# Order of root, reciprocal, table load and weight rounding around the norms of a two-block network

## Chip, core and metric

The kernel runs on one core of a Trainium2 chip. The metric is the device time of one execution in microseconds (us). The engines are called PE (TensorE; PEld is its weight load), DVE (VectorE), ACT (ScalarE), POOL (GpSimd) and SP (SyncE, which here issues most DMAs). Each engine runs its own list of instructions in order, and semaphores tie the lists together.

## What is computed

Two transformer-like blocks on a sequence of 512 tokens of width 1024, all in float32. The first block (differential attention, Fourier mixing and a routed mixture of experts) isn't touched. The second one has two layers; each is a mixer (layer 0: an S5 state-space mixer, layer 1: Mamba-2) and a squared-ReLU MLP, with a modulated RMS norm ahead of each and one at the end:

```python
def _rmsnorm(x, g):
    return x * lax.rsqrt(jnp.mean(x * x, axis=-1, keepdims=True) + NORM_EPS) * g
def _sq_relu_mlp(h, w1, w2):
    a = jax.nn.relu(h @ w1)
    return (a * a) @ w2

for i in range(2):
    sh1, sc1, g1, sh2, sc2, g2 = split(silu(c) @ ada_w[i] + ada_b[i])
    h = _rmsnorm(x, norm_mix_g[i]) * (1 + sc1) + sh1
    y = s5_mixer(h) if i == 0 else ssd_mixer(h)      # Mamba-2; its end: y = groupwise rmsnorm(y * silu(z)) @ w_out
    x = x + g1 * y
    h = _rmsnorm(x, norm_mlp_g[i]) * (1 + sc2) + sh2
    x = x + g2 * _sq_relu_mlp(h, mlp_w1[i], mlp_w2[i])
return _rmsnorm(x, final_norm_g)
```

## The kernel before

Activations lie with features on the 128 partitions: `x`, `h` and the like are eight chunks (KC = 8) of 128 features by T = 512 tokens. Large products of the second block are made of three matmuls for each pair of chunks: weights and activations are each split into a rounded high part and a low rest, and high*high, low*high and high*low are added in PSUM (L739, L742 and L743; L759, L762 and L763 for the first half tile of a pass, which goes chunk by chunk). The high part of a weight tile is made by ACT (`round_half`, one instruction for half a tile, 128x2048, recorded at L1497), the low one by DVE (`split_weight_half`, L2076), which waits for ACT's. A tile has two halves, and there are two tiles in the ring (s = 0, 1); SP loads them as PE frees them.

Norms are numbered k. Norms 5 to 8 belong to the second half: 5 stands ahead of the MLP of layer 0, 6 ahead of the Mamba-2 input projection ("xbc"), 7 ahead of the MLP of layer 1, 8 is the last one. They run so:

- ACT squares the chunks of `x` as DVE finishes them (`norm_squares`, L1503; for norm 5 inside the S5 output loop, L1845, and the last two in `mlp`, L1852). DVE adds the squares of chunks up (`add_square`, L2040).
- PE sums over features in `joined_sum` (L784), then drains and signals `ms_done`.
- ACT takes the root (`norm_root`, L1509) straight from PSUM, 128x128 in size. Ahead of it stands a root of a single column (L1506), the first instruction that needs the table of the root; where another table is in place, a table load is recorded in front of it, at its line.
- DVE takes the reciprocal (`norm_inverse`, L2029), and PE spreads it over the partitions with eight small matmuls (L790).
- DVE scales a chunk (`scaled` in `split_normed`, L2086), ACT adds the shift and rounds it (`norm_shift_rounded`, L1524), DVE makes the low rest (L2097), and PE starts on that chunk. Chunk after chunk follows while PE works.

The weights of the first tile are rounded and split in the same place. ACT's order is: squares, both halves of the tile (`round_weights`), table and root, shifts. DVE's order in `split_normed` is: split of the first half, reciprocal, wait for the spread, scalings; the second half is split behind chunk 4.

In the Mamba-2 output (`m2_out`) the normed values come in four groups of four chunks. DVE scales a group (L2804), ACT copies it rounded (the four copies recorded at L1497), DVE subtracts (L2807, `lo_ready`), and PE uses four chunks of rows for each half tile. ACT rounds the second tile, both halves, ahead of group 1's copies. The order on every engine is written out by hand.

## Time and profile before

| | us |
|---|---|
| median of 3 runs | 2343.35 |
| the runs | 2343.03, 2343.35, 2350.75 |
| the profiled execution | 2343.23 |
| its span | 2341.50 |

The profile is of one execution. The span goes from its first instruction to its last; 1.73 us lie around it. A matmul's duration overlaps the next one's, and ACT and DVE instructions overlap their successors by about 0.1 us, so a start time tells more than an end. In a timeline, what stands in brackets is the engine's idle time ahead of the instruction and the work that ended it. PEclk is the clock granted to PE, 1.00 being full speed (2.4 GHz) and 0.50 half (1.2 GHz).

### The profile page before, as it was taken

What the parts mean: (1) busy time and instruction counts of PE and PEld (TensorE: products, weight loads), DVE (VectorE), ACT (ScalarE), POOL (GpSimd) and SP (SyncE); (2) the same over time, 40 slices, a digit from 0 to 9 for tenths busy, and PEclk for the clock granted to TensorE, in tenths of its full rate; (3) what the DMA queues carried; (4) which work ended last, traced back from release to release, by engine and by line L of the source; (5) the groups of instructions that cost most, each with busy time, mean ns of one, the idle gap of its engine ahead of it and who ended that gap; (6) DMA issues with size and microseconds to landing.
All of it is one profiled execution on the core that took longest, in us unless ns stands there. A gap on an engine that the chain in (4) does not pass through costs nothing.

```text
span 2341.5 us, 23672 instructions
## 1 busy us (share of the span) xinstructions
PE 2092.8 (89%) x9320; PEld 1387.1 (59%) x9320; DVE 1123.0 (48%) x1607; ACT 674.2 (29%) x1029; POOL 162.8 (7%) x172
## 2 busy tenths in 40 slices
PE   6999997987777877979899999899779898999998
PEld 2544443322222226657688888787557686888886
DVE  1866853120111107884465565577684464433434
ACT  3123422110100106213232232243663423322321
POOL 0011101023000023000000000000120000000000
PEclk9999998999999999989899999999889998999999
DMA  9746565999999994212344455223433122322321
GB/s 389 281 145 220 200 256 173 401 429 426 427 428 427 427 390 153 82 63 72 126 171 162 170 172 166 95 90 126 149 105 108 55 90 72 105 93 90 107 90 54
DMA packets 119377, 455.81 MB, mean 195 GB/s; under 512 B 8844, under 2 KB 18096, under 8 KB 104056
## 3 DMA queue, kind: packets, MB, share of 16 engines
q1 hardware_dynamic: 92856, 369.85, 41.6%
q0 software_dynamic: 21312, 76.36, 9.3%
q10 hardware_dynamic: 5120, 8.39, 1.0%
q8 instruction: 60, 0.98, 0.2%
q14 instruction: 29, 0.24, 0.0%
HBM read 436.88 MB, written 21.06 MB: 196 GB/s over the span
## 4 chain that ended last, share of the span: by engine, by line
PE 69%; DMA 18%; DVE 7%; ACT 3%; DVEq 2%; issue 1%; SPq 0%; POOL 0%; ACTq 0%; PEldq 0%; PEld 0%; POOLq 0%
PE PS L739 14%; PE PS L743 14%; PE PS L742 14%; DMA work<-in_w_gu 10%; PE PS L825 4%; PE PS L1111 4%; DMA ring<-in_w_gu 3%; PE PS L1130 3%; DMA work<-in_ada_w_2T 3%; PE PS L954 2%; PE PS L1239 2%; PE PS L759 2%; PE PS L762 2%; PE PS L763 2%; DMA ring<-in_w_in 1%
## 5 line engine op out<-in xcount | busy, mean ns | idle before, releaser
L743 PE MATMUL PS<-work_f32r,work_f32r 128*128 128x512 f32 x1440 | 562.0, 390 | 0.0
L2076 DVE TENSOR_TENSOR ring_f32r<-ring,work_f32r 128x2048 fp32r<-128x2048 f32 x100 | 228.0, 2290 | 167.4 <-ACT work_f32r L1497 167.2
L739 PE MATMUL PS<-work_f32r,work_f32r 128*128 128x512 f32 x768 | 300.7, 392 | 8.0 <-DVE work_f32r L2807 8.0
L743 PEld LDWEIGHTS PS<-work_f32r,work_f32r 128*128 128x128 f32 x1440 | 271.4, 188 | 56.5
L742 PE MATMUL PS<-work_f32r,ring_f32r 128*128 128x512 f32 x768 | 300.0, 391 | 0.0
L1497 ACT ACTIVATE work_f32r<-ring 128x2048 fp32r<-128x2048 f32 x100 | 189.9, 1910 | 315.3 <-DMA ring<-in_mlp_w 246.8
L739 PE MATMUL PS<-h_f32r,work_f32r 128*128 128x512 f32 x672 | 264.0, 393 | 4.0 <-DVE norm_buf L2793 4.0
L742 PE MATMUL PS<-h_f32r,ring_f32r 128*128 128x512 f32 x672 | 262.1, 390 | 0.0
L1111 PE MATMUL PS<-work 128*64 128x512 f32 x752 | 181.8, 631 | 60.0 <-DMA work<-in_w_gu 55.6
L2369 DVE TENSOR_TENSOR work<-work,PS 128x256 f32<-128x256 f32 x32 | 13.5, 421 | 326.3 <-ACT work L1709 326.3
L739 PEld LDWEIGHTS PS<-work_f32r,work_f32r 128*128 128x128 f32 x768 | 145.1, 189 | 38.8 <-issue 8.6
L742 PEld LDWEIGHTS PS<-work_f32r,ring_f32r 128*128 128x128 f32 x768 | 145.0, 189 | 30.3 <-issue 0.2
L1111 PEld LDWEIGHTS PS<-work 128*64 128x64 f32 x752 | 56.9, 144 | 169.6 <-issue 132.1
L739 PEld LDWEIGHTS PS<-h_f32r,work_f32r 128*128 128x128 f32 x672 | 126.4, 188 | 33.5 <-DVE norm_buf L2793 4.9
L742 PEld LDWEIGHTS PS<-h_f32r,ring_f32r 128*128 128x128 f32 x672 | 126.6, 188 | 26.9 <-issue 0.7
L1497 ACT ACTIVATE work<-PS 128x512 f32<-128x512 f32 (+2 forms) x110 | 53.4, 495 | 273.1 <-PE PS L825 90.7
L2612 DVE SCALAR_TENSOR_TENSOR x<-PS,mod,x 128x512 f32<-128x512 f32 x64 | 48.1, 751 | 136.3 <-PE PS L743 136.2
L2605 DVE TENSOR_SCALAR work<-PS 128x512 f32<-128x512 f32 x64 | 44.2, 691 | 122.1 <-PE PS L743 122.0
L1709 ACT ACTIVATE work<-PS 128x256 f32<-128x256 f32 x32 | 12.3, 383 | 306.2 <-PE PS L1111 306.2
L1868 ACT ACTIVATE work_f32r<-work 128x512 fp32r<-128x512 f32 x64 | 40.4, 632 | 176.8 <-DVE work L2605 176.7
L1130 PE MATMUL PS<-work 128*64 128x512 f32 x384 | 87.6, 598 | 1.4 <-ACT work L1497 1.4
L825 PE MATMUL PS<-h,ring 128*128 128x512 f32 x192 | 86.8, 609 | 2.3 <-DMA ring<-in_w_in 2.1
(414 smaller groups left out, 2790.4 us busy)
## 6 DMA issues: line engine op xcount, KB each, us to landing
work<-in_w_gu SPq DMA_DIRECT2D x47, 2048.0 KB, 24.2
ring<-in_mlp_w SPq DMA_DIRECT2D x64, 1024.0 KB, 5.3
work<-in_w_dn SPq DMA_DIRECT2D x24, 2048.0 KB, 27.4
ring<-in_w_gu SPq DMA_DIRECT2D x16, 2048.0 KB, 23.4
work<-in_ada_w_2T POOLq DMA_DIRECT2D x48, 512.0 KB, 3.9
work<-in_ada_w_2T POOLq DMA_DIRECT2D x16, 1536.0 KB, 6.9
ring<-in_m_w_in SPq DMA_DIRECT2D x20, 1024.0 KB, 5.1
work<-in_w_adaT POOLq DMA_DIRECT2D x8, 2048.0 KB, 10.6
```

The lines of the kernel that those rows point to most:

```text
L739: mm = nc.tensor.matmul(PS[:, bank + k, :], f32r(w_of), f32r(hi(c)), start=first and c == 0, stop=False)
L742: nc.tensor.matmul(PS[:, bank + k, :], f32r(wlo), f32r(hi(c)), start=False, stop=False)
L743: mm = nc.tensor.matmul(PS[:, bank + k, :], f32r(w_of), f32r(lo(c)), start=False, stop=last and c == 3)
L759: mm = nc.tensor.matmul(PS[:, bank + k, :], f32r(w_of), f32r(hi[:, c, :]), start=(c == 0), stop=False)
L762: nc.tensor.matmul(PS[:, bank + k, :], f32r(wlo), f32r(hi[:, c, :]), start=False, stop=False)
L763: mm = nc.tensor.matmul(PS[:, bank + k, :], f32r(w_of), f32r(lo[:, c, :]), start=False, stop=False)
L825: mm = nc.tensor.matmul(PS[:, bank, 0:n], cols_of(c), rhs_of(c), start=(c == 0), stop=(c == KC - 1))
L1111: mm = nc.tensor.matmul(PS[CAP * half:CAP * (half + 1), 2 + s, :], xbT[:, slot, 4 * part + c, CAP * s:CAP * (s + 1)], w[:, c, half * 512:( ...
L1130: mm = nc.tensor.matmul(PS[CAP * n:CAP * (n + 1), 5 + s, :], hidT[:, s, k % 2, CAP * (k // 2):CAP * (k // 2 + 1)], w[:, k, n * 512:(n + 1) ...
L1497: return nc.scalar.activation(out, in_, ACT.Copy)
L2076: tt(f32r(ring[:, s, at, :]), ring[:, s, at, :], f32r(tiles[s][:, at, :]), ALU.subtract).then_inc(w_split, 1)
L2612: stt(x[:, n, :], PS[:, n, :], mod2[:, layer, 5 * KC + n:5 * KC + n + 1], x[:, n, :], ALU.mult, ALU.add).then_inc(mlp_added, 1)
```

## The change

A helper `root_table` on ACT holds the one-column root. It is called ahead of the squares for norms 5, 6, 7 and 8 instead of just ahead of the root. For norms 5, 6 and 7 only the first half of the first weight tile is rounded ahead of the root and the second half behind it. On DVE the split of the first half moves from ahead of the reciprocal to between the reciprocal and the wait for the spread (`meanwhile`). In the Mamba-2 output, the second tile's first half is rounded ahead of group 1's copies as before, its second half behind them. No instruction is added or removed, and nothing that is computed changes.

```diff
--- before.py
+++ after.py
@@ -1502,9 +1502,13 @@
                         act.wait_ge(ready, count + c + 1)
                     nc.scalar.activation(sq[:, c, :], src[:, c, :], ACT.Square).then_inc(sq_ready, 1)
 
+            def root_table(k):
+                nc.scalar.activation(sm[:, 32 + k:33 + k], ones[:, 0:1], ACT.Sqrt)
+
             def norm_root(k, n):
-                nc.scalar.activation(sm[:, 32 + k:33 + k], ones[:, 0:1], ACT.Sqrt)
-                if k >= 5:
+                if k < 5:
+                    root_table(k)
+                else:
                     act.wait_ge(ms_done, k + 2)
                     nc.scalar.activation(std_q, PS[:, 6, 0:P], ACT.Sqrt, scale=1.0 / D, bias=eps5).then_inc(std_ready, 1)
                     return
@@ -1846,14 +1850,16 @@
 
             def mlp(layer, k_norm):
                 first = PAIRS[f"mlp{layer}"][0]
+                root_table(k_norm)
                 if layer == 0:
                     for c in range(KC - 2, KC):
                         act.wait_ge(glu_used, c + 1)
                         nc.scalar.activation(glu_sq[:, c, :], x[:, c, :], ACT.Square).then_inc(sq_ready, 1)
                 else:
                     norm_squares(x, h, x5_ready)
-                round_weights(first, 0)
+                round_half(first, 0, 0)
                 norm_root(k_norm, T)
+                round_half(first, 0, 1)
                 norm_shift_rounded(k_norm, mlp_h_lo, mod2[:, layer, 3 * KC:4 * KC])
 
                 def quarter(i, last):
@@ -1876,9 +1882,11 @@
 
 
             first = PAIRS["xbc"][0]
+            root_table(6)
             norm_squares(x, h, mlp_added, 8 + 3 * KC)
-            round_weights(first, 0)
+            round_half(first, 0, 0)
             norm_root(6, T)
+            round_half(first, 0, 1)
             norm_shift_rounded(6, xbc_h_lo, mod2[:, 1, 0:KC])
 
             def conv_out(i, last):
@@ -2002,15 +2010,18 @@
             first = PAIRS["m2_out"][0]
             for g in range(M2_G):
                 if g == 1:
-                    round_weights(first, 1)
+                    round_half(first, 1, 0)
                 if g == 2:
                     group_root(3)
                 for n in range(4 * g, 4 * g + 4):
                     act.wait_ge(yn_ready, n + 1)
                     copy(f32r(xs[:, n, :]), y_lo(n)).then_inc(y_hi_ready, 1)
+                if g == 1:
+                    round_half(first, 1, 1)
             for s in range(2):
                 round_weights(first + 1, s)
             mlp(1, 7)
+            root_table(8)
             norm_squares(x, h, mlp_added, 8 + 7 * KC)
             norm_root(8, T)
 
@@ -2023,10 +2034,12 @@
                 dve.wait_ge(ms_done, k + 1)
                 ts(var[:, 0:n], PS[:, NORM_BANKS[k], 0:n], 1.0 / D, eps, ALU.mult, ALU.add).then_inc(var_ready, 1)
 
-            def norm_inverse(k, n):
+            def norm_inverse(k, n, meanwhile=None):
                 dve.wait_ge(std_ready, k + 1)
                 if k >= 5:
                     nc.vector.reciprocal(inv_q, std_q).then_inc(rstd_ready, 1)
+                    if meanwhile is not None:
+                        split_weight_half(meanwhile, 0, 0, 0)
                     dve.wait_ge(mod_evac_and_spread, k - 3)
                     return PS[:, 7, :]
                 nc.vector.reciprocal(rstd[:, 0:n], rstd[:, 0:n])
@@ -2085,8 +2098,7 @@
                 def scaled(c):
                     stt(lo[:, c, :], x[:, c, :], scale[:, c:c + 1], inverse, ALU.mult, ALU.mult).then_inc(xn_ready, 1)
 
-                split_weight_half(name, 0, 0, 0)
-                inverse = norm_inverse(k, T)
+                inverse = norm_inverse(k, T, name)
                 scaled(0)
                 for c in range(KC):
                     if c + 1 < KC:
```

## Rows read from the trace of the kernel before

**Rows 1.** The page: busy time by engine (part 1), and the chain by engine (part 4).
```profile
PE 2092.8 (89%) x9320; PEld 1387.1 (59%) x9320; DVE 1123.0 (48%) x1607; ACT 674.2 (29%) x1029; POOL 162.8 (7%) x172
...
PE 69%; DMA 18%; DVE 7%; ACT 3%; DVEq 2%; issue 1%; SPq 0%; POOL 0%; ACTq 0%; PEldq 0%; PEld 0%; POOLq 0%
```

**Rows 2.** Windows view (us; busy and count by engine; PEclk, DMA share, GB/s).
```profile
1146.10:1160.54 14.44, 3.16 (x24) 2.44 (x25) 9.58 (x12) 9.07 (x11) 1.62 (x2) 0.60 0.59 218
...
1160.54:1511.60 351.06, 351.06 (x1536) 290.13 (x1536) 201.47 (x240) 102.00 (x107) 10.82 (x14) 0.99 0.47 159
...
1511.60:1522.76 11.16, 2.74 (x26) 2.16 (x25) 7.45 (x11) 5.95 (x7) 0.00 (x0) 0.62 0.00 0
...
1864.30:1872.24 7.94, 0.00 (x1) 0.03 (x1) 6.70 (x11) 7.89 (x12) 0.00 (x0) 0.81 0.00 0
...
1964.80:1975.98 11.18, 2.76 (x26) 2.16 (x25) 7.00 (x8) 5.95 (x7) 0.00 (x0) 0.65 0.00 0
```

**Rows 3.** Timeline at norm 5 (start, duration, engine, line; [idle before, releaser]).
```profile
1147.23 0.62 ACT L1852 ACTIVATE work<-x 128x512 f32<-128x512 f32 x1
...
1148.85 0.63 ACT L1852 ACTIVATE work<-x 128x512 f32<-128x512 f32 x1 [1.00 <-DVE x L2577]
...
1148.91 1.46 DVE L2040 TENSOR_TENSOR work<-work 128x512 f32<-128x512 f32 x2
...
1149.39 3.69 ACT L1497 ACTIVATE work_f32r<-ring 128x2048 fp32r<-128x2048 f32 x2
...
1150.52 1.08 PE L784 MATMUL PS<-work,ones 128*32 128x128 f32 x16 [4.43 <-DVE work L2040]
...
1153.10 1.28 ACT L1506 ACT_TABLE_LOAD   x1
...
1154.51 0.35 ACT L1509 ACTIVATE norm_buf<-PS,sm 128x128 f32<-128x128 f32 x1
...
1158.01 1.41 DVE L2086 SCALAR_TENSOR_TENSOR work<-x,gain,PS 128x512 f32<-128x512 f32 x2 [2.17 <-PE PS L790]
```

**Rows 4.** Timeline at norm 6: ACT, PE and DVE around the root.
```profile
1512.98 3.69 ACT L1497 ACTIVATE work_f32r<-ring 128x2048 fp32r<-128x2048 f32 x2
...
1513.24 0.65 PE L784 MATMUL PS<-h,ones 128*32 128x128 f32 x16 [1.63 <-DVE h L2040]
...
1514.90 2.29 DVE L2076 TENSOR_TENSOR ring_f32r<-ring,work_f32r 128x2048 fp32r<-128x2048 f32 x1 [1.09 <-ACT work_f32r L1497]
...
1516.67 0.35 ACT L1509 ACTIVATE norm_buf<-PS,sm 128x128 f32<-128x128 f32 x1
...
1517.11 0.94 DVE L2029 RECIPROCAL norm_buf<-norm_buf 128x128 f32<-128x128 f32 x1
```

**Rows 5.** Timeline at norm 7, ACT.
```profile
1966.20 3.69 ACT L1497 ACTIVATE work_f32r<-ring 128x2048 fp32r<-128x2048 f32 x2
```

**Rows 6.** Timeline at norm 8, ACT.
```profile
2329.59 0.37 ACT L1509 ACTIVATE norm_buf<-PS,sm 128x128 f32<-128x128 f32 x1 [0.81 <-PEq L786]
```

**Rows 7.** Timeline in the Mamba-2 output: ACT, DVE and PE.
```profile
1878.29 1.92 ACT L1497 ACTIVATE work_f32r<-ring 128x2048 fp32r<-128x2048 f32 x1 [5.48 <-DMA ring<-in_m_w_out]
...
1880.76 2.50 DVE L2807 TENSOR_TENSOR work_f32r<-work,work_f32r 128x512 fp32r<-128x512 f32 x4 [2.70 <-ACT work_f32r L1497]
...
1888.07 0.79 PE L739 MATMUL PS<-work_f32r,work_f32r 128*128 128x512 f32 x1
```

**Rows 8.** Windows view around falls and rises of PEclk.
```profile
1166.00:1167.00 1.00, 1.00 (x6) 0.82 (x5) 1.00 (x1) 0.00 (x0) 0.00 (x0) 0.93 0.25 94
...
1514.00:1514.50 0.50, 0.00 (x0) 0.00 (x0) 0.00 (x0) 0.50 (x1) 0.00 (x0) 0.79 0.00 0
...
1527.00:1528.00 1.00, 1.00 (x3) 0.75 (x3) 1.00 (x2) 0.72 (x1) 0.00 (x0) 0.53 1.02 397
...
1876.00:1877.00 1.00, 1.00 (x5) 0.82 (x5) 1.00 (x3) 0.00 (x0) 0.00 (x0) 0.95 1.06 414
...
1981.00:1982.00 1.00, 1.00 (x4) 0.81 (x3) 1.00 (x1) 0.12 (x1) 0.00 (x0) 0.54 0.45 172
```

## Prediction

> **What bounds the kernel now.** I first read the page's busy shares and its chain: PE is busy 89% of the span and holds 69% of the chain that ended last, while DVE and ACT are busy 48% and 29% [rows 1]. So an edit on ACT or DVE counts only where PE stands idle for it. I then laid stretches over the second half (the windows view). From 1160.54 to 1511.60, the whole first MLP, PE is busy for all 351.06 us at clock 0.99; nothing saved on ACT or DVE there reaches the end [rows 2]. The pass that ends at 1864.30 and the Mamba-2 output that starts at 1872.24 are 7.94 us apart. Between such stretches lie the norms too: from the last matmul of a projection to the first of the next pass 14.44 us (norm 5), 11.16 us (norm 6) and 11.18 us (norm 7), in which PE works only some 3 us [rows 2]. These gaps are what the change touches, and since PE runs without a pause behind them, a gap that gets shorter by a microsecond should end the kernel a microsecond earlier.
>
> Third, the timeline inside the gaps. At norm 5 ACT squares the last two chunks, rounds both halves of a weight tile (3.69 us), loads an activation table (1.28 us) and only then takes the root, at 1154.51 [rows 3]. The sum that the root reads was finished at 1150.52 + 1.08 = 1151.60 [rows 3]. So 2.9 us of the gap are ACT's order, not data. At norm 6 the sum is done at 1513.24 + 0.65 = 1513.89 and the root starts at 1516.67, right where two roundings that began at 1512.98 end; there DVE too is at work on the weight split (1514.90 to 1517.19), which comes before the reciprocal in its order, so that the reciprocal waits for both engines until 1517.11 [rows 4]. Norm 7 repeats norm 6: again two roundings of 3.69 us together from 1966.20, ahead of the root [rows 5]. The root of norm 8 waits for PE's sum itself (0.81 us of idle, ended by PE), with no rounding ahead of it [rows 6].
>
> **Part 1: root ahead of the second rounding, reciprocal ahead of the split (norms 6 and 7).** Before the root stands one rounding instead of two. One is half of 3.69 us, 1.85 us. The root of norm 6 can then start at 1512.98 + 1.85 = 1514.83, later than the sum's 1513.89, so ACT is still what comes last and the whole 1.85 us goes [rows 4]. DVE: if only ACT's order changed, the split would still hold the reciprocal to 1517.11 and nothing would be won; moved behind it, the reciprocal (0.94 us) can follow the root (0.35 us) at once [rows 4]. Its new place is while PE spreads the reciprocal; DVE idled 2.17 us for that at norm 5, ahead of its first scaling [rows 3]. The split takes 2.29 us [rows 4], so it ends 0.1 us late, or 0.2 with the hand-over; I take 0.1 for each of the three norms, 0.3 in all. The second rounding now runs after the root and is cover for nobody: ACT is next wanted when the first chunk has been scaled, more than 3 us after the root, and the rounding is 1.85 us. Its split on DVE comes behind the fifth chunk, as before. PE's first matmul needs the first split, done before the first scaling. No DMA is issued by the moved steps, and SP's and POOL's queues are passed by nothing. Gain 1.85 at norm 6, 1.85 at norm 7.
>
> **Part 2: the same at norm 5, with the table load moved.** The load (1.28 us) goes ahead of the last two squares. It can start when ACT is free of the square before them, about 1147.3 (the next one began at 1147.23) [rows 3]. With the small root that pulls it in (about 0.1) it is over at 1148.75. The two squares, 0.62 and 0.63 us, then end at about 1149.35 and 1149.9 in place of 1147.85 and 1149.48 [rows 3]. Most of this delay is hidden: before, ACT stood idle 1.00 us between them. Who waits for them? DVE's two additions start at 1148.91 and take 1.46 us; the second reads the first of these squares and starts near 1149.64, so it is not late. PE's sum begins at 1150.52, released by these additions, and needs the last square only in its second half [rows 3]. So the sum still ends at 1151.60. ACT's one rounding runs from 1149.85 to 1151.7. Root at 1151.7 in place of 1154.51: gain 2.8 us, of which 1.85 is the rounding, 1.3 + 0.1 the load and its root, less 0.4 for the later squares. From there both ACT and the sum are within 0.1 us of each other; nothing more could be won by order.
>
> The price of the load is what this case shows: it starts 0.02 us after the rounding ends (1149.39 + 3.69 = 1153.08) and the real root starts 0.13 us after its end [rows 3]. The Trainium skill (page "ScalarE: Activation LUTs", section "What ACT_TABLE_LOAD costs") gives 1283 ns for the load and about 1380 ns of drain on top, 2.66 us for a switch. The trace has the first number and not the second. By the page's sum the squares of norm 5 would come 1.4 us later still; that is a rival below.
>
> **Part 3: small roots of norms 6, 7 and 8.** They pull in no load there; they move into idle time of ACT ahead of the squares. The 0.1 us they took at norms 6 and 7 lay inside the rounding sum; at norm 8 the root waits for PE anyway [rows 6]. I cost them at nothing; if a small root fell between two squares it would cost 0.2 us.
>
> **Part 4: the Mamba-2 output.** The four copies of group 1 go ahead of the rounding of the second half of a tile, which idled 5.48 us for its DMA and started at 1878.29 [rows 7]. The subtractions of that group, 1880.76 to 1883.26 on DVE, come some 2.5 us earlier; the rounding comes up to half a microsecond later if the copies are still at work when the DMA lands. PE wants the subtracted rows at 1888.07 and starts there with no idle time ahead of it [rows 7]: 4.8 us of slack before, 7 after. Cost and gain 0; without this cover, were PE early, at most 2.5 us of gain; a loss has no place to come from, because the half whose rounding moves is the last of the four that PE works through, and the second of them starts at 1888.07.
>
> **Sum.** 2.8 + 1.85 + 1.85 - 0.3 = 6.2 us. The profiled execution took 2343.23 us (span 2341.50, 1.73 around it), 0.12 below the median of 2343.35. 2343.2 - 6.2 = 2337.0 us, or 0.26% less.
>
> **The clock.** PE's granted clock is 1.00 (2.4 GHz) until about 2.7 us after a dense pass has ended, then 0.50 (1.2 GHz): at norm 6 it falls at 1514.3 [rows 8]. It is back at 1166.0, 1528.0 and 1982.0, that is 5.5, 5.2 and 6.0 us after the first matmul of the pass (1160.54, 1522.76, 1975.98), and at 1876.05, 3.8 us after PE's restart at 1872.24 in the Mamba-2 output [rows 2, 8]. At half clock a pass loses about half of the stretch. These delays differ though the work is alike, so each can come out between 3.8 and 6.0 us once everything is shifted: from -0.8, -0.7 and -1.1 to +0.25, +0.4 and 0 us, and up to +1.1 in the Mamba-2 output. That gives about -2.6 to +1.8 around the sum, so 2334.4 to 2338.8 is the forecast's own range.
>
> **Rivals.** (a) The shorter gap keeps the clock up. For: the gaps shrink by 1.9 to 2.9 us. Against: at norm 6 the clock has fallen before the spread starts, and 9.4 us of gap are left. If it held, three delays of about 5.5 us at half rate would go, 8.3 us: 2328.7. Chance 0.03. (b) The load is not hidden at norm 5 (the change then not doing what it says there): it is met again behind the squares, or holds the squares up for a second 1.28 us beyond its recorded time. Either way 1.3 to 1.4 of the 2.8 us go: 2338.4. Against it: at norm 6 the root follows square and roundings with no load between them [rows 4], so these share a table. Chance 0.07. (c) The reciprocal's gain is eaten by the split, because it slows down beside PE's reads or PE waits for it: with the split fully behind the scaling's start each norm would lose up to 2.3 us, and 6.2 would shrink to nothing only if all three did; partly, 2339 to 2342. Chance 0.06. (d) Slower than before: the half-clock stretches lengthen. Everything behind norm 5 is shifted, and the Mamba-2 middle has many short bursts of PE. At half a microsecond lost for each, it decides from 12.4 us of added half clock; the four restarts in the rows can give only 3.5 of them, the rest would have to come from stretches whose rows show none of this. It would read 2344 to 2347. Chance 0.04.
>
> **How the numbers follow.** Forecast 2337.0 with chance 0.80; (a) 0.03, (b) 0.07, (c) 0.06, (d) 0.04. To hold 8 in 10 the range takes the clock's bounds and reaches to (b) and part of (c): 2333.5 to 2340.5. About 0.5% (11.7 us) is what a measurement of this kernel can tell from no change. Faster by more needs under 2331.6, of the cases only (a), and a little for what no case names: 0.04. Slower by more needs over 2355: 0.02. Within 0.5%: 0.94.
>
> **What would show it.** At norm 5 the table load stands ahead of the two last squares and the root starts near 1151.7; at norms 6 and 7 the root starts one rounding after the last square, and in the three gaps the split stands between reciprocal and first scaling with no idle time beside it. The gaps read 11.7, 9.4 and 9.4 us. The Mamba-2 output starts its four copies ahead of the last rounding and PE goes on as before. The prediction is wrong if the gaps shrink and the span does not (PE not the bound behind them), if the first scaling waits for the split by more than 0.3 us, or if the sum of norm 5 comes later than before.

## The result and the profile after

The changed kernel takes 2333.03 us (median of 9 runs, 2329.43 to 2339.13), the kernel before 2345.50 us in the runs beside it (9 runs, 2339.91 to 2350.75). The ratio is 0.9946, with a 95% interval of 0.9933 to 0.9960: 0.54% less. Forecast were 2337.0 us, a range of 2333.5 to 2340.5, and 0.26% less. The time is half a microsecond under the range, and the gain over the kernel before is twice the forecast one.

The profiled execution took 2333.20 us, its span 2331.5. The page of the changed kernel: busy time by engine, chain by engine.

```profile
PE 2092.1 (90%) x9320; PEld 1386.0 (59%) x9320; DVE 1124.3 (48%) x1607; ACT 674.4 (29%) x1029; POOL 162.6 (7%) x172
...
PE 69%; DMA 14%; DVE 6%; ACT 3%; issue 3%; DVEq 2%; POOLq 1%; POOL 1%; SPq 0%; ACTq 0%; PEldq 0%; PEld 0%
```

Nothing shows at this level: PE's busy time is 2092.1 us against 2092.8 [rows 1], 10 us of span are gone, and they were idle or half-clock time. The windows view shows where. The stretches are three of [rows 2], from the last matmul of a pass to the first of the next one.

```profile
1146.10:1157.98 11.88, 3.41 (x26) 2.44 (x25) 9.69 (x12) 9.06 (x11) 1.62 (x2) 0.64 0.53 192
...
1508.70:1517.86 9.16, 1.89 (x25) 1.35 (x25) 7.30 (x11) 5.86 (x6) 0.00 (x0) 0.82 0.00 0
...
1958.30:1967.60 9.30, 2.83 (x26) 2.17 (x25) 6.94 (x8) 5.86 (x6) 0.00 (x0) 0.68 0.00 0
```

The three gaps read 11.88, 9.16 and 9.30 us against 14.44, 11.16 and 11.18. These stretches begin at round marks; measured from the first matmul of the sum (L784) to the first matmul of the pass (L759) they are 7.21, 7.45 and 7.57 us in place of 10.02, 9.52 and 9.51. In sum 6.8 us are gone from the gaps. The middle lines of the timeline at norm 5 (ACT, PE and DVE; start, duration):

```profile
1147.62 1.28 ACT L1506 ACT_TABLE_LOAD   x1
...
1149.02 1.13 ACT L1857 ACTIVATE work<-x 128x512 f32<-128x512 f32 x2
...
1150.06 1.89 ACT L1497 ACTIVATE work_f32r<-ring 128x2048 fp32r<-128x2048 f32 x1
...
1150.77 1.08 PE L784 MATMUL PS<-work,ones 128*32 128x128 f32 x16 [4.42 <-DVE work L2053]
...
1151.93 0.37 ACT L1513 ACTIVATE norm_buf<-PS,sm 128x128 f32<-128x128 f32 x1
...
1153.21 2.23 DVE L2089 TENSOR_TENSOR ring_f32r<-ring,work_f32r 128x2048 fp32r<-128x2048 f32 x1
...
1155.46 1.41 DVE L2099 SCALAR_TENSOR_TENSOR work<-x,gain,PS 128x512 f32<-128x512 f32 x2
```

Here is what was described: the table load (1147.62) stands ahead of the squares (1149.02), PE's sum still begins at its old distance, the root comes at 1151.93, right behind the sum's end (1150.77 + 1.08 = 1151.85), the reciprocal follows at 1152.34, and the split (1153.21) lies between it and the first scaling (1155.46). All of this execution lies 0.25 us later than the one of [rows 3], so the root is at the forecast 1151.7. Norm 6:

```profile
1510.14 1.89 ACT L1497 ACTIVATE work_f32r<-ring 128x2048 fp32r<-128x2048 f32 x1
...
1510.41 0.64 PE L784 MATMUL PS<-h,ones 128*32 128x128 f32 x16 [1.63 <-DVE h L2053]
...
1511.94 0.35 ACT L1513 ACTIVATE norm_buf<-PS,sm 128x128 f32<-128x128 f32 x1
...
1512.33 0.95 DVE L2040 RECIPROCAL norm_buf<-norm_buf 128x128 f32<-128x128 f32 x1 [1.34 <-ACT norm_buf L1513]
...
1513.19 2.23 DVE L2089 TENSOR_TENSOR ring_f32r<-ring,work_f32r 128x2048 fp32r<-128x2048 f32 x1
...
1513.33 1.16 PE L790 MATMUL PS<-norm_buf,mats_sb 128*128 128x128 f32 x8 [2.28 <-DVE norm_buf L2040]
...
1515.34 1.40 DVE L2099 SCALAR_TENSOR_TENSOR work<-x,gain,PS 128x512 f32<-128x512 f32 x2
```

The root starts 1.80 us behind the rounding's start, not 3.69 [rows 4]. And one thing is new: PE's spread takes 1.16 us, not 2.08 as in the kernel before. The clock was still up. The spread was over at 1514.49, and the first scaling waited 0.85 us longer, for the split. The windows around falls and rises of PEclk in the changed kernel:

```profile
1163.00:1164.00 1.00, 1.00 (x6) 0.82 (x5) 1.00 (x1) 0.12 (x1) 0.00 (x0) 1.00 0.43 166
...
1514.00:1515.00 1.00, 0.49 (x5) 0.30 (x3) 1.00 (x1) 0.09 (x1) 0.00 (x0) 0.79 0.00 0
...
1521.00:1522.00 1.00, 1.00 (x5) 0.82 (x4) 1.00 (x2) 0.68 (x1) 0.00 (x0) 0.80 1.02 389
...
1971.00:1972.00 1.00, 1.00 (x3) 0.73 (x3) 1.00 (x3) 0.41 (x1) 0.00 (x0) 0.52 0.96 367
```

At norm 6 the clock fell at 1514.6, just behind the spread; in the kernel before it fell at 1514.3 with the spread still 3.8 us away. It came back at 1521.4, 3.5 us after the first matmul (1517.86), where it had taken 5.2. At norm 5 the delay is 5.0 in place of 5.6, at norm 7 4.4 in place of 5.9.

By stages the 10.07 us between the two spans are:

| stage | before | after | gain |
|---|---|---|---|
| to the sum of norm 5 | 1150.52 | 1150.77 | -0.25 |
| sum of norm 5 to first matmul | 10.02 | 7.21 | 2.81 |
| first MLP, to the sum of norm 6 | 352.70 | 352.43 | 0.27 |
| sum of norm 6 to first matmul | 9.52 | 7.45 | 2.07 |
| Mamba-2, to the first group sum (L1458) | 270.29 | 268.78 | 1.51 |
| gate projection and output, to the sum of norm 7 | 173.42 | 173.39 | 0.03 |
| sum of norm 7 to first matmul | 9.51 | 7.57 | 1.94 |
| second MLP, to the sum of norm 8 | 352.88 | 352.11 | 0.77 |
| sum of norm 8 to the end | 12.66 | 11.75 | 0.91 |

The last one is again a spread at full clock (2.08 us in the kernel before), with nothing on DVE to hide what it saves:

```profile
2321.85 1.16 PE L790 MATMUL PS<-norm_buf,mats_sb 128*128 128x128 f32 x8 [1.50 <-DVE norm_buf L2040]
```

So the second half gained 10.3 us: 6.8 in the gaps, 3.5 outside them, where no instruction was moved.

### The profile page after: what moved, and what is told of

Its sections match the earlier page's. It is cut to its first block, busy times and chain, and to the rows that moved or that the text cites. A ratio compares the mean times of both kernels' runs of the same rounds, so it can differ in the third digit from the quotient of the medians.

```text
span 2331.5 us, 23672 instructions
## 1 busy us (share of the span) xinstructions
PE 2092.1 (90%) x9320; PEld 1386.0 (59%) x9320; DVE 1124.3 (48%) x1607; ACT 674.4 (29%) x1029; POOL 162.6 (7%) x172
## 4 chain that ended last, share of the span: by engine, by line
PE 69%; DMA 14%; DVE 6%; ACT 3%; issue 3%; DVEq 2%; POOLq 1%; POOL 1%; SPq 0%; ACTq 0%; PEldq 0%; PEld 0%
PE PS L739 14%; PE PS L743 14%; PE PS L742 14%; DMA work<-in_w_gu 7%; PE PS L825 5%; PE PS L1111 3%; DMA ring<-in_w_gu 3%; PE PS L1130 2%; DMA work<-in_ada_w_2T 2%; PE PS L1239 2%; PE PS L954 2%; PE PS L759 2%; PE PS L762 2%; PE PS L763 2%; DMA ring<-in_w_in 1%
## 5 line engine op out<-in xcount | busy, mean ns | idle before, releaser
L1111 PE MATMUL PS<-ring,work 128*64 128x512 f32 x256 | 64.5, 651 | 26.5 <-DMA ring<-in_w_gu 25.3
```

What stands on the lines that cost most here:

```text
L1111: mm = nc.tensor.matmul(PS[CAP * half:CAP * (half + 1), 2 + s, :], xbT[:, slot, 4 * part + c, CAP * s:CAP * (s + 1)], w[:, c, half * 512:( ...
```

## The experiments

**How far runs lie apart.** First the two kernels again, and two parts of the change alone, side by side on one chip. `before_again` and `after_again` have no edit.

> The kernel before, unchanged, timed against itself. By every theory the ratio is 1.000; what it shows is how far two sets of runs of one program lie apart, and, in its profile, how far the stages of one program move between two executions: the mixture of experts up to 900 us, the falls and rises of PE's clock behind 1149 us. Theory S (the steps gain 6.8 us, the rest of the measured 12.6 us is scatter of the part before 1150 us and of the clock's phase) expects the delays from the first matmul of a pass to the return of the clock to differ from 5.5, 5.2 and 6.0 us by a microsecond or two. Theory C (the shorter gap itself brings the clock back sooner) expects the same delays as before within 0.5 us.

> The changed kernel, unchanged, once more. Theory S: 7 to 9 us under the kernel before (ratio 0.9963 to 0.997), and in the profile the three gaps of 11.9, 9.1 and 9.3 us again, but the delays to the return of the clock (5.0, 3.6 and 4.4 us in the first profile) drawn anew between 3.6 and 6 us. Theory C: 11 to 13 us under it (ratio 0.9945 to 0.9953) with delays again below those of before at all three norms.

Measured: the kernel before against itself 1.0013 (1.0000 to 1.0026), so two sets of runs of one program differ by 3 us here. The changed kernel 0.9971 (0.9957 to 0.9985), 2333.06 us against 2341.66 (33 runs); that is theory S's value, in microseconds (8.6) and, at its edge, as a ratio. The changed kernel's median came out at 2333.0 twice; it is the kernel before that read 2345.5 in one comparison and 2341.7 in the other. Over all runs beside these and the later comparisons, from several sessions, its median is 2342.9 (94 runs), that of the changed one 2333.0 (20 runs): 9.8 us.

The profiles are sharper than the times. In eleven executions of kernels that share all code ahead of norm 5 the sum of norm 5 began between 1148.1 and 1156.7 us: that is the scatter of the times, and it lies in the first block, which the change doesn't touch. From that sum to the end it was 1191.01, 1191.08 and 1191.03 us with the old norms (the last with the Mamba-2 output changed), and 1180.69 and 1180.57 us in the changed kernel. The delays to the clock's return repeated too: 5.6, 5.2 and 5.9 us twice in the kernel before, 4.9 to 5.0, 3.5 and 4.4 twice in the changed one. The expectation that they would be drawn anew (theory S) fell for these kernels. One limit goes with it: in ten of the eleven executions the clock fell 1.4 to 1.5 us ahead of the sum of norm 5, in one (that of DVE's order alone, below) 0.6 us ahead, though the code ahead of norm 5 is the same in all of them. From here on "second half" means the time from the first matmul of the sum of norm 5 to the end of the span, and it is compared to a tenth of a microsecond.

**Norm 5 alone.** Its ACT order and split as in the changed kernel; norms 6 and 7 and the Mamba-2 output go back to the old order (norm 6 shown; the small root of norm 8 stays where the change put it):

```diff
-            root_table(6)
             norm_squares(x, h, mlp_added, 8 + 3 * KC)
-            round_half(first, 0, 0)
+            round_weights(first, 0)
+            root_table(6)
             norm_root(6, T)
-            round_half(first, 0, 1)
...
-                inverse = norm_inverse(k, T, name)
+                if k != 5:
+                    split_weight_half(name, 0, 0, 0)
+                inverse = norm_inverse(k, T, name if k == 5 else None)
```

> Only norm 5 has the new order (table load ahead of its last squares, root behind one rounding, split behind the reciprocal); norms 6 to 8 and the Mamba-2 output as before. Both theories: the gap of norm 5 shrinks by 2.8 us, those of norms 6 and 7 stay at 11.2. Theory S: 2.8 us in all, ratio 0.9988, give or take the scatter of the clock. Theory C: 2.8 us and about half a microsecond of clock.

Measured: ratio 0.9985 (0.9972 to 0.9997). Sum to first matmul 7.21 us at norm 5, 9.51 at norms 6 and 7; second half 1187.65 us, 3.4 less than before. The gap gave 2.81. The rest is as large as theory C had it, and 0.4 of it follows from the clock's return (5.0 in place of 5.6 us at norm 5, 4.9 in place of 5.2 at norm 6).

**The Mamba-2 output alone.** In the kernel before:

```diff
                 if g == 1:
-                    round_weights(first, 1)
+                    round_half(first, 1, 0)
...
+                if g == 1:
+                    round_half(first, 1, 1)
```

> Only the order in the Mamba-2 output is changed; all norms as before. Both theories: ratio 1.000; DVE's subtractions for group 1 come about 2.5 us earlier and PE's matmuls follow without a pause at the same distance as before. A third theory, M (the Mamba-2 output carries a part of the gain that the steps of the norms don't), expects 2 us or more, ratio 0.999 or less, and a shorter stretch from the end of the gate projection to the last matmul of the output.

Measured: ratio 1.0009 (0.9999 to 1.0019), second half 1191.03 us, the same as without it. Theory M fell. In the changed kernel the order is there, and ACT is idle on either side of it: its timeline, copies of group 1 first, then the second half's rounding.

```profile
1869.71 2.62 ACT L1497 ACTIVATE work_f32r<-work 128x512 fp32r<-128x512 f32 x4 [3.29 <-DVE work L2816]
...
1872.23 1.90 ACT L1497 ACTIVATE work_f32r<-ring 128x2048 fp32r<-128x2048 f32 x1
```

**Norms 6 and 7 alone** (the reverse selection of the norm 5 experiment: `if k == 5` where that has `if k != 5`).

> Only norms 6 and 7 have the new order; norm 5 and the Mamba-2 output as before. In the profiles so far the second half repeats to 0.1 us from one execution to the next (1191.0 us from the sum of norm 5 to the end in three kernels that leave all of it, or all but the Mamba-2 output, as it was; 1180.6 in two executions of the changed kernel). Theory R (each gap gives its own microseconds, and on top of that the clock of the pass behind it comes back at an instant that doesn't follow the first matmul, so that a pass gets back about half of what the first matmul and half of what the return of the clock gained): gap 5 stays 14.8 us, gaps 6 and 7 are 9.5 us, and from the sum of norm 5 to the end 1184 to 1186 us, 5 to 7 less than before. Theory A (every gap gives its own microseconds and nothing else): 4.0 less, 1187.0.

Measured: ratio 0.9973 (0.9962 to 0.9984). Both stretches 7.56 us in place of 9.5, so 3.9 us from the gaps; but the second half is 1187.81 us, only 3.2 less. This is below theory A's 4.0 and far from theory R's 5 to 7. The clock's return at norm 6 came with 3.8 us of delay in place of 5.2, which is a gain; in the Mamba-2 stage behind it, though, the time to the first group sum rose from 270.29 to 271.75, of which the stage behind it took 0.6 back. The gaps did as said, the total did not follow either theory.

**ACT's order alone, DVE's order alone.** From the changed kernel, DVE put back:

```diff
-                inverse = norm_inverse(k, T, name)
+                split_weight_half(name, 0, 0, 0)
+                inverse = norm_inverse(k, T)
```

> ACT as in the changed kernel (small root and table load ahead of the squares, root behind one rounding, the Mamba-2 output's order too), DVE as before: the split of the first half stays ahead of the reciprocal. The prediction's step that both moves are needed expects no gain at norms 6 and 7: there the split, 1.9 us behind the rounding's start and 2.3 us long, ends 4.2 us behind that start and the reciprocal follows as before, gaps 11.4 to 11.5 us. At norm 5 the rounding ends at 1.9 us behind its start too, the split 2.2 later: the reciprocal 0.4 to 0.7 us earlier than before, gap 14.2 to 14.5. The rival, that ACT's order is the gain and DVE's place doesn't matter, expects gaps of 12.0, 9.5 and 9.6 as in the changed kernel.

Measured at norm 6:

```profile
1511.07 1.89 ACT L1497 ACTIVATE work_f32r<-ring 128x2048 fp32r<-128x2048 f32 x1
...
1512.87 0.35 ACT L1513 ACTIVATE norm_buf<-PS,sm 128x128 f32<-128x128 f32 x1
...
1512.99 2.29 DVE L2089 TENSOR_TENSOR ring_f32r<-ring,work_f32r 128x2048 fp32r<-128x2048 f32 x1 [1.09 <-ACT work_f32r L1497]
```

The root comes 1.80 us behind the rounding's start in place of 3.69, so 1.9 us earlier, and DVE's split starts 0.12 us behind the root and holds the reciprocal for its 2.29 us. Sum to first matmul is 9.51 us at norms 6 and 7, as before. At norm 5 it is 9.08 in place of 10.02, 0.9 us of gain where 0.4 to 0.7 were expected. The other half, DVE as changed and ACT as before:

```diff
-                split_weight_half(name, 0, 0, 0)
-                inverse = norm_inverse(k, T)
+                inverse = norm_inverse(k, T, name)
```

> DVE as in the changed kernel (reciprocal ahead of the split of the first half), ACT and the Mamba-2 output as before. The other half of the pair to the kernel with ACT's order alone: the root of norms 6 and 7 still comes behind two roundings, where DVE's split had just ended, so the reciprocal is no earlier. Gaps 14.8, 11.5 and 11.5 as before, within 0.1. If DVE's order were a gain by itself, below 11.4.

```profile
1512.79 3.69 ACT L1497 ACTIVATE work_f32r<-ring 128x2048 fp32r<-128x2048 f32 x2
...
1516.48 0.35 ACT L1509 ACTIVATE norm_buf<-PS,sm 128x128 f32<-128x128 f32 x1
...
1516.87 0.95 DVE L2029 RECIPROCAL norm_buf<-norm_buf 128x128 f32<-128x128 f32 x1 [3.23 <-ACT norm_buf L1509]
```

The root waits for two roundings again, and the reciprocal follows it at once with nothing won. Sum to first matmul: 10.17, 9.46 and 9.46 us. So at norms 6 and 7 neither order is worth anything alone and both together are worth 2: two engines had been equally late there. At norm 5 ACT's order alone is worth 0.9, DVE's alone nothing (0.15 us of loss), both 2.8. Yet these two kernels, with 0.9 and 0 us out of their gaps, had second halves of 1187.84 and 1188.41 us, 3.2 and 2.6 less than before. What the clock adds is as large as the steps, and it needs no shorter gap: at norm 6, with its 9.51 us as before, ACT's order alone had the clock back after 3.9 us in place of 5.2. That goes against theory C as a rule. At norm 5 of DVE's order alone the delay was 2.8 us in place of 5.6, in a gap that was 0.15 us longer. The windows at the fall and the return there:

```profile
1150.00:1151.00 1.00, 0.00 (x0) 0.00 (x0) 0.93 (x2) 1.00 (x2) 0.31 (x1) 0.93 0.00 0
...
1164.00:1165.00 1.00, 1.00 (x5) 0.82 (x4) 1.00 (x2) 0.40 (x2) 0.00 (x0) 0.74 0.80 174
```

The fall, at 1150.86, is the odd one named above: it lies 0.6 us ahead of the sum (1151.50). It came ahead of anything that this kernel changes, so its 2.6 us can belong to this one execution and not to its order; there is only the one profile of it.

**The table load.** The changed kernel with the small root of norm 5 back behind the rounding:

```diff
-                root_table(k_norm)
+                if k_norm != 5:
+                    root_table(k_norm)
...
                 round_half(first, 0, 0)
+                if k_norm == 5:
+                    root_table(k_norm)
                 norm_root(k_norm, T)
```

> The changed kernel, but at norm 5 the small root with its table load stays between the first rounding and the root, as before; everything else as in the changed kernel. The prediction's price of the load: it puts 1.3 + 0.1 us back on ACT's chain and takes 0.5 us of delay off the squares, so the root comes 1.0 to 1.1 us later and the gap of norm 5 is 13.0 us in place of 12.0. With a drain of 1.38 us on top of a load the gap would be 14.4. Behind the gap theory R leaves it to the return of the clock what the pass makes of it.

```profile
1152.53 1.90 ACT L1497 ACTIVATE work_f32r<-ring 128x2048 fp32r<-128x2048 f32 x1
...
1153.66 1.08 PE L784 MATMUL PS<-work,ones 128*32 128x128 f32 x16 [4.42 <-DVE work L2056]
...
1154.44 1.28 ACT L1506 ACT_TABLE_LOAD   x1
...
1155.85 0.35 ACT L1513 ACTIVATE norm_buf<-PS,sm 128x128 f32<-128x128 f32 x1
```

The load starts where the rounding ends, takes 1.28 us, and the root starts 0.13 us behind it. Sum to first matmul is 8.38 us against 7.21: 1.17 for the load's place, expected 1.0 to 1.1. The switch of 2.66 us that the Trainium skill gives (page "ScalarE: Activation LUTs", section "What ACT_TABLE_LOAD costs") would have made it 1.4 more, 9.8 us; the measurement decides for 1.28 us, and no drain of that size stands behind the load here. The second half of this kernel is 1184.37 us, 3.7 more than the changed kernel's, for a gap that is longer by 1.2.

**Where the rest comes from.** At half clock matmuls of one kind follow each other by 0.43 us, at full clock by 0.23. Two pairs from the timeline of the kernel before:

```profile
1523.34 0.63 PE L762 MATMUL PS<-h_f32r,ring_f32r 128*128 128x512 f32 x1
...
1523.77 0.63 PE L763 MATMUL PS<-work_f32r,work_f32r 128*128 128x512 f32 x1
...
1504.65 0.39 PE L739 MATMUL PS<-work_f32r,work_f32r 128*128 128x512 f32 x1
...
1504.88 0.39 PE L742 MATMUL PS<-work_f32r,ring_f32r 128*128 128x512 f32 x1
```

So a microsecond less at half clock is worth 0.47 us, as the delays of the first profile bear out: 5.6 to 5.0 at norm 5 is 0.26 us (the first MLP gained 0.27), 5.9 to 4.4 at norm 7 is 0.74 (the second MLP gained 0.77). In all eleven executions without fillers both MLPs take 350.1 us and 0.47 of the delay, within 0.1 us: 351.39 us for the shortest delay (2.84) and 352.88 for 5.94. 350.1 is also what they take at full clock, in the filler kernels below.

In the Mamba-2 stage the gain up to the first group sum is 1.51 us. Laid side by side matmul by matmul, the two kernels are 0.77 us apart once the clock is back at norm 6, and still so at 1683.63 (before) and 1677.95 (after). There a burst of matmuls begins, which runs at half clock from 1684.96 on in the kernel before and at full clock in the changed one. Two of its lines in each, before first:

```profile
1684.66 1.73 PE L1419 MATMUL PS<-work 128*64 128x128 f32 x16
...
1686.32 2.08 PE L1430 MATMUL PS<-work 128*128 128x512 f32 x2
```

```profile
1678.98 1.09 PE L1419 MATMUL PS<-work 128*64 128x128 f32 x16
...
1680.00 1.12 PE L1430 MATMUL PS<-work 128*128 128x512 f32 x2
```

The burst is 1.6 us shorter. PE's waits for DVE behind it let 0.6 of that through by 1698.68 (1692.38 after), and the clock's next return adds 0.1. Elsewhere half clock falls into waits: from the clock's return to the first group sum there are 41.0 us of it in the changed kernel against 37.6 in the kernel before, and the difference costs nothing.

To see what sets the delay, the root of norm 7 alone was made late by a known time, in the changed kernel:

```diff
                 else:
+                    if k == 7:
+                        for n in range(10):
+                            nc.scalar.activation(sm[:, n:n + 1], ones[:, 0:1], ACT.Sqrt)
                     act.wait_ge(ms_done, k + 2)
```

> The changed kernel, with ten roots of a single column more on ACT ahead of the root of norm 7 alone (about 0.1 us each), so that this root comes later than in the changed kernel by a known and small time. Up to the sum of norm 7 all as there. Both theories: gap 7 is longer by about 1.0 us (10.6). Theory R: the clock comes back at the same instant as before (the delay from the first matmul is 3.4 instead of 4.4 us), so the pass gets half of it back and the sum of norm 8 is later by 0.5 us, not by 1.0. Theory A: the delay stays 4.4 us and the sum of norm 8 is later by the whole 1.0 us.

```profile
1958.46 0.64 PE L784 MATMUL PS<-h,ones 128*32 128x128 f32 x16 [1.63 <-DVE h L2056]
...
1959.99 1.02 ACT L1514 ACTIVATE sm<-ones 128x1 f32<-128x1 f32 x10
...
1966.95 0.79 PE L759 MATMUL PS<-h_f32r,work_f32r 128*128 128x512 f32 x1 [2.57 <-DVE work_f32r L2112]
```

```profile
1970.00:1971.00 1.00, 1.00 (x5) 0.77 (x5) 1.00 (x3) 0.73 (x1) 0.00 (x0) 0.82 0.89 324
```

The ten small roots took 1.02 us, the first matmul comes 8.49 us behind the sum in place of 7.57, 0.92 later. The clock came back at 1970.4, 11.9 us behind the sum of norm 7; in the changed kernel it was 1972.0 - 1960.03, the same 11.9. And the sum of norm 8 was 360.18 us behind that of norm 7 against 359.68: half a microsecond for a delay of 0.92. The return does not follow the first matmul of the pass, at least over this microsecond, and the pass gets back half of what its start lost. This is theory R's expectation; theory A fell for the passes. Norm 5 shows the same over a longer way: with 7.21, 8.38 and 9.08 us from sum to first matmul (changed kernel, late table load, ACT's order alone) the clock came back 12.2 us behind the sum each time. With 10.02 us it came back 15.6 us behind it. So the return stays where it is, and then jumps.

**With the clock held up.** PE's gaps filled with small matmuls on constants into a bank that is free then. In the short version:

```diff
+            def busy(n, bank=0):
+                for _ in range(n):
+                    nc.tensor.matmul(PS[:, bank, 0:P], eye, ones[:, 0:P], start=True, stop=True)
...
                 pe.drain().then_inc(ms_done, 1)
+                busy({5: 5, 6: 8, 7: 8, 8: 0}[k])
...
                 mm.then_inc(mod_evac_and_spread, 1)
+                if k < 8:
+                    busy(9)
...
             pe.wait_ge(glu_used, 5)
+            busy(17)
             joined_sum(5, glu_sq)
...
             pe.wait_ge(ovar_ready, HEADS + M2_G - 1)
+            busy(23, 1)
```

> The changed kernel with PE kept at work in its gaps by small matmuls on constants (128x128, float32, into a PSUM bank that nobody reads then; their results are never used): 30 ahead of the sum of norm 5, 13 between sum and spread and 14 behind the spread of norms 5 to 7, 38 ahead of the first product of the Mamba-2 output, 8 between sum and spread of norm 8. It prices the clock. If the clock stays at 1.00, the delays of 5.0, 3.5 and 4.4 us at half clock and that of the Mamba-2 output (3.8) go: 0.47 of 16.7 us is 7.8 us, and the spreads take 1.16 in place of 2.08 us, which the split on DVE hides almost wholly. From the sum of norm 5 to the end 1172 to 1174 us in place of 1180.6, in the ratio another 0.003. If work of this kind doesn't hold the clock up, or the small matmuls come in the way of sum, spread or first product: no gain, or up to 3 us of loss.

> The fill kernel with fewer small matmuls. In its trace one such matmul on full clock takes 0.235 us (two records of 0.12), so that 14 of them lasted 3.3 us where the gap had 2.6 and held up the first product, and 38 lasted 9 us where the Mamba-2 output had 6. Now 17 ahead of the sum of norm 5, 5, 8 and 8 between sum and spread, 9 behind the spreads, none at norm 8, 23 ahead of the Mamba-2 output. Expected: the clock stays at 1.00 as in the fill kernel, the stretch from sum to first product is that of the changed kernel (7.2, 7.45 and 7.5 us instead of 7.7), PE starts on the Mamba-2 output 2 us sooner, and from the sum of norm 5 to the end 1172 to 1173 us (fill kernel 1175.7, changed kernel 1180.6, before 1191.0). If the gaps now left lower the clock again, 1178 to 1181. Ratio to the kernel before 0.992 to 0.994.

Measured: `fill` 0.9950 (0.9930 to 0.9969), second half 1175.72 us; it held up sums and products where it was too long (7.7 us from sum to first matmul). `fill_short` 0.9944 (0.9924 to 0.9964), second half 1174.23, 6.4 less than the changed kernel; 1172 to 1173 had been expected. Its timeline at norm 6 (L778 are the fillers), and both MLPs in the windows view:

```profile
1507.83 0.64 PE L788 MATMUL PS<-h,ones 128*32 128x128 f32 x16 [1.63 <-DVE h L2062]
...
1508.59 2.05 PE L778 MATMUL PS<-ones,mats_sb 128*128 128x128 f32 x16
...
1510.75 1.16 PE L795 MATMUL PS<-norm_buf,mats_sb 128*128 128x128 f32 x8
...
1515.37 0.49 PE L759 MATMUL PS<-h_f32r,work_f32r 128*128 128x512 f32 x1 [1.45 <-DVE work_f32r L2118]
```

```profile
1157.74:1507.60 349.86, 348.47 (x1536) 288.37 (x1536) 202.50 (x242) 102.33 (x110) 10.82 (x14) 1.00 0.48 162
...
1960.00:2310.00 350.00, 348.64 (x1543) 288.68 (x1541) 148.70 (x147) 103.47 (x110) 0.00 (x0) 1.00 0.26 87
```

The clock is 1.00 from the first matmul on in both MLPs. It is up too at the restarts of norm 6 and of the Mamba-2 output, and still falls in the Mamba-2 middle, where nothing was filled. The MLPs take 350.1 us from first matmul to the next sum in place of 352.4 and 352.1. Whether this kernel beats the changed one in time is not decided by the times: 2331.0 us (6 runs) and 2333.0 (20 runs), with intervals that overlap. The second half says yes, by 6 us.

The last run puts the question the other way round: old order, clock held up.

```diff
                 pe.drain().then_inc(ms_done, 1)
+                busy({5: 17, 6: 17, 7: 17, 8: 0}[k])
...
```

> The kernel before, its order untouched, with PE kept at work in its gaps by small matmuls on constants as in the short fill kernel (17 ahead of the sum of norm 5, 17 between sum and spread of norms 5 to 7, since these stretches are longer in the old order, 9 behind the spreads, none at norm 8, 23 ahead of the Mamba-2 output). With the clock at 1.00 on both sides of every gap, old order against new order shows what the order alone is worth. If the gain beyond the gaps (10.4 us in the second half against 6.8 in the three gaps) is the clock's return, it is gone here: the passes of the two MLPs take 350.1 us each as in the short fill kernel, and from the sum of norm 5 to the end 1174.2 + 6.8 = 1181.0 us, give or take 1 us for the bursts of the Mamba-2 middle. If the new order gives more than its gaps by some other way, 1183 to 1185.

```profile
1510.04 5.68 PE L778 MATMUL PS<-ones,mats_sb 128*128 128x128 f32 x34
...
1513.15 0.95 DVE L2038 RECIPROCAL norm_buf<-norm_buf 128x128 f32<-128x128 f32 x1
...
1515.56 1.06 PE L795 MATMUL PS<-norm_buf,mats_sb 128*128 128x128 f32 x8
```

```profile
1159.20:1509.00 349.80, 348.46 (x1536) 288.13 (x1536) 202.47 (x242) 102.17 (x108) 10.82 (x14) 1.00 0.47 160
```

Measured: ratio 0.9946 (0.9928 to 0.9964): without touching the order, fillers bring as much as the change does. Second half 1179.97 us, where 1181.0 give or take 1 had been expected. It is 5.7 more than the short fill kernel; 6.8 had been expected. The difference is all in the gaps: sum to first matmul 9.20, 9.91 and 8.59 us against 7.05, 7.54 and 7.44, 5.7 in all, while the two MLPs take 350.1 us in both and the Mamba-2 stages, from the first matmul behind norm 6 to the sum of norm 7, 439.41 us against 439.33. So with the clock up at the restarts the order gives its gaps and nothing else. For the Mamba-2 middle this holds in sum only: the clock fell there in both (0.74 on average from 1657 to 1757 us in the old order, 0.83 in the new one), the first group sum came 1.7 us later in the old order, and the stage behind it made that up. The numbers aren't clean at norm 6: there the clock was at half from 1510.4 to 1513.8, the fillers took 5.68 us (4.06 at norm 7) and lasted until 1515.6, 1.5 us past the reciprocal's end (1513.15 + 0.95). So up to 1.5 of the 5.7 us are the fillers' own. What remains, some 4.2, is less than 6.8, since a spread at full clock makes the old order 0.9 us shorter, while in the new one the split hides that.

## Why the prediction was wrong

The steps, in the prediction's own order:

- **Part 1** (root ahead of the second rounding, 1.85 us each at norms 6 and 7, less 0.1 for the split): right in mechanism, measured 2.07 and 1.94. That both moves were needed is shown by the two kernels with one each. The 0.1 us of the small root was on the chain after all (1.89 us instead of 1.85), the reciprocal follows the root 0.05 us sooner than it had followed the split, and the charge for a late split was not due: in its new place it takes 2.23 us, and the scaling started as soon as the spread was over at norm 7. At norm 6, where the spread was short, the split was what came last, by 0.85 us. That is one of the prediction's own signs of being wrong (the first scaling waits for the split by more than 0.3 us). It was met because the spread ran at full clock, not because the split was slow, and the gap still came out 0.25 us shorter than forecast.
- **Part 2** (norm 5, 2.8 us): 2.81. The root came where it was put, and the load's place is worth 1.17 of it, where the forecast counted 1.0 (1.4 less 0.4 for the later squares). Rival (b), a load not hidden, is out: it lies ahead of the squares in the trace, with 1.28 us.
- **Part 3** (small roots, nothing): right at norm 8, 0.04 us of gain each at 6 and 7.
- **Part 4** (Mamba-2 output, nothing): right, shown by the kernel with that part alone. The subtractions came 2.8 us earlier, counted from PE's start on the output, and the moved rounding 0.3 us later.
- **The sum** was therefore 0.6 us short: 6.8 in place of 6.2.
- **The clock** is the step that failed. It was given -2.6 to +1.8 us around the sum, from delays between 3.8 and 6.0 us, and gave 3.5 on the side of gain. Three things were wrong in it. The lower bound of the delay was taken from the one shortest restart in the rows; norm 6 came out at 3.5, and the experiments have 2.8. Only four restarts were counted, and the stage from norm 6 to the first group sum gained 1.5 us, of which its pass explains 0.8 (1.6 us of delay at 0.47); the other 0.7 was made at one burst of the Mamba-2 middle, whose rows the prediction had not read. In the experiments without fillers this stage moved between 268.7 and 271.9 us. And rival (a) was dismissed because the clock falls ahead of the spread; at norms 6 and 8 of the changed kernel it fell behind it, and at norm 8 this alone gave 0.9 us. By terms the 3.5 us are 0.3 and 0.8 from the MLPs' restarts, 0.8 from that behind norm 6, 0.7 from the burst and 0.9 from the last spread.
- **The base.** The sum was taken off 2343.2 us. Over all runs the kernel before has a median of 2342.9, so this term was 0.3 us off, and the first block scatters by 8.6 us from one execution to another (eleven profiles). The 0.54% of the first comparison are in part this scatter: 10.3 us are what the second halves show, 9.8 us all runs together, and 12.5 the first comparison.

Rivals (c) and (d) didn't come about. What sets the clock's return in a given kernel stays open. The runs show that it repeated in the five executions of the kernel before, the one with the Mamba-2 output changed, and the changed kernel, that in one other execution the clock's fall lay 0.8 us nearer to the sum of norm 5 before any changed code ran, that the return does not follow the first matmul by a fixed time, and that with it the second half can move by 3.7 us for 1.2 us of gap (the table load's experiment). In seven kernels with gaps shorter by 0, 0.9, 2.8, 3.9, 5.7, 5.9 and 6.8 us the second half was shorter by 2.6, 3.2, 3.4, 3.2, 6.7, 9.9 and 10.3 us. With the clock held up at the restarts the extra was gone. That the clock is the whole of the 3.5 us is shown for the two MLPs and the last spread. For the 0.7 us of the Mamba-2 middle it is read from one pair of traces: the burst at half clock is there, how much of it the waits for DVE pass on was not tested by an edit.

## What to carry to other kernels

Where two engines are equally late for a third, moving work on one of them gives nothing and moving both gives all of it: follow both chains to the common step. In a PE-bound kernel with gaps, price a shorter gap by its own microseconds, and give the clock behind it a range of its own, as wide as half of the restart delays of all stages that follow, short bursts included. And where the part that isn't touched scatters by more than the gain, compare the touched part between fixed marks in the profile; in the five executions named it repeated to 0.1 us, while the start of the second half moved by 8.6 over the eleven.

## What the runs showed of the hardware

PE's clock was at 0.50 for 2.8 to 6.0 us after the restart of a pass behind norms 5 to 7, and each of those microseconds cost the pass 0.47. Two executions of one kernel agreed in the delay to 0.15 us. Moving the first matmul by up to 1.9 us left the return where it was, and by 2.8 it jumped. Small matmuls on constants (128x128, float32, 0.22 to 0.24 us each at full clock) between sum, spread and first product kept it at 1.00 in both MLPs; in the old order that alone was worth as much as the whole change (11.0 us of the second half against 10.3). Where the clock fell while they ran (norm 6 in the old order), they held up the spread behind them. The table load took 1.28 us, and the root, with a small one ahead of it, started 0.13 us behind it.
